# Hybrid decoder block on one core: reordered last down-projection group with interleaved stores, and a new opening around the meta tokens

## What is computed

```python
hs = concatenate([meta_tokens, x])                                   # (272, 2048)
hs = hs + 0.5 * swiglu(rmsnorm(hs, ffn1_norm), w_gate, w_up, w_down)   # d_ff 5632
hs = hs + token_mixing(rmsnorm(hs, mix_norm), w_in, ..., w_out)
hs = hs + 0.5 * swiglu(rmsnorm(hs, ffn2_norm), w_gate, w_up, w_down)
out = rmsnorm(hs, final_norm)[16:]                                   # (256, 2048)
```

## Time and profile before

| | us |
|---|---|
| median of 3 runs | 1904.35 (1903.69 to 1904.44) |
| the profiled execution | 1904.94 |
| its span, first to last event | 1902.9 |
| PE busy in it | 1878.2 |
| DVE busy | 1121.6 |
| ACT busy | 922.6 |
| POOL busy | 22.2 |
| moved by DMA | 342.21 MB |

### The profile page before, as it was taken

How to read it: one execution, slowest core, us unless ns; L and a number is a source line. 1 busy time by engine, 2 the same in 40 slices (tenths; PEclk the granted TensorE clock), 3 DMA queues, 4 the chain that set the end, 5 groups by cost and what they waited for, 6 DMA issues and landing times.

```text
span 1902.9 us, 31295 instructions
## 1 busy us (share of the span) xinstructions
PE 1878.2 (99%) x12639; PEld 1751.7 (92%) x12639; DVE 1121.6 (59%) x1212; ACT 922.6 (48%) x1176; POOL 22.2 (1%) x33
## 2 busy tenths in 40 slices
PE   8999999999999999999999999999999999999997
PEld 7999999999999999999998788888888888888886
DVE  6555555555554544468898998555566555544443
ACT  6434433443443444359888665444444444433443
POOL 4000000000000000000000000000000000000000
PEclk9999999999999999999999999999999999999999
DMA  6655555555555565555655566666656666666663
GB/s 196 189 176 176 170 173 176 172 172 175 176 171 174 177 174 172 175 175 169 186 182 168 163 191 191 193 187 188 188 176 187 188 196 189 212 187 187 189 189 121
DMA packets 283387, 342.21 MB, mean 180 GB/s; under 512 B 10656, under 2 KB 223746, under 8 KB 283169
## 3 DMA queue, kind: packets, MB, share of 16 engines
q1 hardware_dynamic: 282960, 340.83, 58.7%
q0 software_dynamic: 288, 0.19, 0.0%
q10 hardware_dynamic: 64, 0.14, 0.0%
HBM read 339.02 MB, written 2.10 MB: 179 GB/s over the span
## 4 chain that ended last, share of the span: by engine, by line
PE 96%; DVE 2%; ACT 1%; DMA 0%; issue 0%; ACTq 0%; DVEq 0%
PE ps L451 20%; PE ps L446 17%; PE ps L444 17%; PE ps L445 17%; PE ps L452 10%; PE ps L547 4%; PE ps L545 4%; PE ps L546 4%; DVE w_lo L806 1%; PE ps L404 0%; PE ps L555 0%; DMA m_tok<-in_meta_tokens 0%; DVE res L939 0%; DVE ln_sum L1003 0%; DVE res L932 0%; DVE y_f L921 0%
## 5 line engine op out<-in xcount | busy, mean ns | idle before, releaser
L806 DVE TENSOR_TENSOR w_lo<-raw,w_hi 128x1024 fp32r<-128x1024 f32 x640 | 784.4, 1227 | 660.7 <-ACT w_hi L609 658.9
L609 ACT ACTIVATE w_hi<-raw 128x1024 fp32r<-128x1024 f32 x640 | 676.5, 1059 | 862.7 <-PE ps L446 493.2
L444 PE MATMUL ps<-x_both,w_hi 128*128 128x272 f32 (+1 forms) x1920 | 555.2, 289 | 0.0
L446 PE MATMUL ps<-x_both,w_lo 128*128 128x272 f32 (+1 forms) x1920 | 554.3, 289 | 0.0
L445 PE MATMUL ps<-x_both,w_hi 128*128 128x272 f32 (+1 forms) x1920 | 551.8, 287 | 0.0
L451 PE MATMUL ps<-x_both,w_hi 128*128 128x512 f32 x1536 | 537.0, 393 | 0.5 <-DVE w_lo L806 0.5
L452 PE MATMUL ps<-x_both,w_lo 128*128 128x256 f32 x1536 | 430.9, 281 | 0.0
L445 PEld LDWEIGHTS ps<-x_both,w_hi 128*128 128x128 f32 x1920 | 362.6, 189 | 0.1
L444 PEld LDWEIGHTS ps<-x_both,w_hi 128*128 128x128 f32 x1920 | 361.9, 188 | 0.1
L446 PEld LDWEIGHTS ps<-x_both,w_lo 128*128 128x128 f32 x1920 | 361.8, 188 | 0.0
L451 PEld LDWEIGHTS ps<-x_both,w_hi 128*128 128x128 f32 x1536 | 288.3, 188 | 66.6 <-DVE w_lo L806 0.9
(11 more groups left out here) (129 smaller groups left out, 1074.2 us busy)
## 6 DMA issues: line engine op xcount, KB each, us to landing
raw<-in_ffn_w_gate SPq DMA_DIRECT2D x176, 512.0 KB, 3.7
raw<-in_ffn_w_up SPq DMA_DIRECT2D x176, 512.0 KB, 3.6
raw<-in_ffn_w_down SPq DMA_DIRECT2D x176, 512.0 KB, 3.8
raw<-in_w_in SPq DMA_DIRECT2D x80, 512.0 KB, 3.5
raw<-in_w_out SPq DMA_DIRECT2D x32, 512.0 KB, 4.7
x_tok<-in_x SPq DMA_DIRECT2D x4, 512.0 KB, 9.5
out_y<-o_tok SPq DMA_DIRECT2D x8, 256.0 KB, 3.6
gain_tok<-in_final_norm SPq DMA_DIRECT2D x1, 1024.0 KB, 4.6
```

What stands on the lines that cost most here:

```text
L444: pe.matmul(dst, w_high, act_high, start=first, stop=False)
L446: return pe.matmul(dst, w_low, act_high, start=False, stop=last)
L609: act.activation(w_hi[s][:, :], raw[s][:, :], ACT.Copy).then_inc(hi_ready, 1)
L806: dve.tensor_tensor(w_lo[s][:, :], raw[s][:, :], w_hi[s][:, :].bitcast(F32), ALU.subtract).then_inc(lo_ready, 1)
```

## The change

Two places change. At the opening the meta tokens are loaded by two DMAs at the head of SP's queue into 128 partitions (`m_rows`, chunk and token together) and turned by two transposes; x is turned two chunks at a time (`turn_pair`), four chunks before the first projection matmul and the other twelve after blocks 0, 1 and 3; block 0 is loaded and split in two halves; x's four quarters are issued before blocks 0, 2 and 4; PE runs 16 matmuls of the ones tile in three bursts (`keep_warm`); the opening group's matmuls run chunk by chunk; squares are taken of the untransposed x by ACT with an accumulator and spread on a diagonal by DVE; the parameter loads wait for x's second quarter and are turned after block 5. In the last group of `down2` the last four blocks are run for token half 0 first and then for half 1; each half has its own variance, root and scaling; half 0 is stored in two pieces of 512 KB by SP, half 1 in four of 256 KB, two by SP and two by ACT. The early Sqrt is gone. Declarations of semaphores are left out below, long removed parts too (they stand above), and indentation is reduced.

```diff
+x_sums, meta_sum = tok[:, 0:3, :].rearrange("p s h -> p h s"), tok[:, 3, 0:1]
...
-m_tok = at("m_tok", a_at + 4 * HALVES * D, [P, D])
+m_rows = at("m_rows", a_at + 4 * HALVES * D, [P, HALVES, P])
...
 out_pieces = [slice(g * BANK, (g + 1) * BANK) for g in range(G_D)]
-start_squares = [buffer[:, j, :] for buffer in (sq, t1, t2) for j in range(2)]
+wide_pieces = [slice(g * 2 * BANK, (g + 1) * 2 * BANK) for g in range(G_D // 2)]
+HALF_BLOCK = slice(0, BLOCK // 2), slice(BLOCK // 2, BLOCK)
...
+    for h in range(HALVES):
+        meta_half = meta_tokens[:, h * (D // 2):(h + 1) * (D // 2)]
+        sp.dma_start(m_rows[:, h, :],
+                     meta_half.rearrange("t (c p) -> c t p", p=P)).then_inc(meta_loaded, 16)
...
+    def load_first(src):
+        dst = raw[0][:, :].rearrange("p (c n) -> p c n", c=4)
+        for half in range(2):
+            sp.dma_start(dst[:, 2 * half:2 * half + 2, :],
+                         src[:, 2 * half:2 * half + 2, :]).then_inc(first_loaded[half], 16)
...
-                if phase == "gu1" and isinstance(g, int) and g == 0 and i < 4:
-                    load_x(i)
+                if phase == "gu1" and isinstance(g, int) and g == 0:
+                    for q in {0: (0,), 2: (1,), 4: (2, 3)}.get(i, ()):
+                        load_x(q)
                 src = rows[i % 2][i // 2, :, :, bass.ds(g * 256 + (col_a, col_b)[i % 2], 256)]
-                load(phase, g, i, src, 256)
+                if phase == "gu1" and isinstance(g, int) and g == 0 and i == 0:
+                    load_first(src)
+                else:
+                    load(phase, g, i, src, 256)
...
-    for i, cols in enumerate(out_pieces):
...
+    for i in range(2):
+        sp.wait_ge(o_scaled, 2 * i + 2)
+        sp.dma_start(out[0, 0:P, wide_pieces[i]], o_tok[:, 0, wide_pieces[i]]).then_inc(stored, 16)
+    for i in range(2):
+        sp.wait_ge(o_scaled, SET + i + 1)
+        sp.dma_start(out[0, P:2 * P, out_pieces[i]], o_tok[:, 1, out_pieces[i]]).then_inc(stored, 16)
+    sp.wait_ge(stored, 16 * 6)
 @block.gpsimd
...
+    pool.wait_ge(x_loaded[1], 16)
...
-    pool.wait_ge(sq_ready["start"], 1)
...
-    def turn_x(c, bank):
...
+    def turn_pair(q):
+        if q % 2 == 0:
+            pe.wait_ge(x_loaded[q // 2], 16)
+        if q >= 3:
+            pe.wait_ge(emptied, 2 * (q - 2))
+        for c in (2 * q, 2 * q + 1):
+            for h in range(HALVES):
+                at_col = c % 2 * SEQ + h * P
+                m = pe.transpose(ps[:, 4 + q % 3, at_col:at_col + P], x_tok[:, h, c * P:(c + 1) * P],
+                                 ident[:, :])
+        m.then_inc(x_turned, 2)
     def start_between(i):
-        if i == 1:
+        if i in (0, 1, 3):
+            for q in {0: (2, 3), 1: (4, 5), 3: (6, 7)}[i]:
+                turn_pair(q)
+        if i == 5:
             pe.wait_ge(par_loaded, 16 * (len(rows0) + 4))
-            pe.wait_ge(emptied, 5)
+            pe.wait_ge(emptied, KD)
...
-            for c in (8, 9, 10, 11):
...
+    pe.wait_ge(ones_set, 1)
+    def keep_warm(n):
+        for _ in range(n):
+            pe.matmul(ps[:, 0, 0:P], ones[:, :], ones[:, :], start=True, stop=True)
+    keep_warm(7)
...
-    pe.transpose(ps[:, 7, 0:KD], gain_rows[:, :], ident[0:KD, 0:KD]).then_inc(gain_turned, 1)
...
+    pe.transpose(ps[:, 3, 0:KD], gain_rows[:, :], ident[0:KD, 0:KD]).then_inc(gain_turned, 1)
+    pe.wait_ge(meta_loaded, 16 * HALVES)
+    for h in range(HALVES):
+        m = pe.transpose(ps[:, 7, h * P:(h + 1) * P], m_rows[:, h, :], ident[:, :])
+    m.then_inc(meta_turned, 1)
+    keep_warm(5)
+    for q in (0, 1):
+        turn_pair(q)
+    keep_warm(4)
...
     def start_group(phase, g):
-        if phase == "gu1" and isinstance(g, int) and g == 0:
-            pe.wait_ge(emptied, SET)
-        else:
+        if phase != "gu1" or not isinstance(g, int) or g > 0:
...
     def square_sums(norm, phase):
-        pe.wait_ge(sum_ready[norm], KD)
+        pe.wait_ge(sum_ready[norm], 5 if norm == "start" else KD)
...
+                if norm == "start":
+                    pe.wait_ge(par_ready, 4)
...
-                start_block(phase, g, i)
-                for j in range(2):
-                    for c in range(4):
+                opening = norm == "start" and first_group
+                if opening and i == 0:
+                    pe.wait_ge(first_lo, 1)
+                else:
+                    start_block(phase, g, i)
+                for j, c in ([(j, c) for c in range(4) for j in range(2)] if opening
+                             else [(j, c) for j in range(2) for c in range(4)]):
...
+                        if opening and i == 0 and c == 2 and j == 0:
+                            start_block(phase, g, i)
...
         pe.wait_ge(emptied, banks_before("gu2", G_FF - 1) if g < G_D // 2 else banks_before("down2", 0))
-        for i in range(N_DOWN):
...
+        def half_block(i, h):
+                s = slot("down2", g, i)
...
-                if g == G_D - 1 and i == N_DOWN - 1 and h == 0:
-                    m.then_inc(tile_done, 1)
+                return m
+        split = N_DOWN - RING if g == G_D - 1 else N_DOWN
+        for i in range(split):
+            start_block("down2", g, i)
+            if g == 0:
+                pe.wait_ge(alo_ready["gu2"], i + 1)
+            for h in range(HALVES):
+                m = half_block(i, h)
...
+        if split < N_DOWN:
+            for h in range(HALVES):
+                for i in range(split, N_DOWN):
+                    if h == 0:
+                        start_block("down2", g, i)
+                    m = half_block(i, h)
+                m.then_inc(tile_done, 1)
    ...
-    act.dma_start(m_tok[0:META, :], meta_tokens).then_inc(x_loaded[4], 16)
...
-        act.wait_ge(raw_loaded[s], 16 * turn(phase, g, i) + 16)
+        act.wait_ge(raw_loaded[s], 16 * turn(phase, g, i) + (16 if s else 0))
...
-        act.wait_ge(emptied, t + 1 if norm == "start" else banks_before(norm, 0) + t + 1)
+        act.wait_ge(emptied, 2 * (t // 2) + 2 if norm == "start" else banks_before(norm, 0) + t + 1)
...
+    def square_x(h, half):
+        act.wait_ge(x_loaded[2 * half + 1], 16)
+        act.activation(t12[:, :, :].rearrange("p a t -> p (a t)")[:, 0:D // 2],
+                       x_tok[:, h, half * (D // 2):(half + 1) * (D // 2)], ACT.Square,
+                       accum_out=x_sums[:, h, half:half + 1]).then_inc(x_squared, 1)
     act.wait_ge(gain_turned, 1)
-    act.activation(gain1[:, :], ps[:, 7, 0:KD], ACT.Copy).then_inc(gain_ready, 1)
+    act.activation(gain1[:, :], ps[:, 3, 0:KD], ACT.Copy).then_inc(gain_ready, 1)
     act.wait_ge(gain_ready, 1)
-    for q in range(4):
+    act.wait_ge(first_loaded[0], 16)
+    act.activation(w_hi[0][:, HALF_BLOCK[0]], raw[0][:, HALF_BLOCK[0]], ACT.Copy).then_inc(first_hi, 1)
+    act.wait_ge(meta_ready, 1)
+    for t in (0, 1):
+        operand("gu1", "start", t)
+    act.wait_ge(first_loaded[1], 16)
+    act.activation(w_hi[0][:, HALF_BLOCK[1]], raw[0][:, HALF_BLOCK[1]], ACT.Copy).then_inc(hi_ready, 1)
+    for t in (2, 3):
+        operand("gu1", "start", t)
+    high("gu1", 0, 1)
+    for q in range(1, 4):
...
-        high("gu1", 0, 2 * q + 1)
...
+        if q == 3:
+            high("gu1", 0, 7)
         if q == 1:
-            act.wait_ge(par_turned, 4)
...
+            act.wait_ge(meta_loaded, 16 * HALVES)
+            act.activation(t12[:, 0, 0:HALVES * P], m_rows[:, :, :].rearrange("p h n -> p (h n)"),
+                           ACT.Square, accum_out=meta_sum).then_inc(x_squared, 1)
+            act.wait_ge(x_squared, 1)
+            square_x(0, 0)
+        if q == 2:
+            act.wait_ge(x_squared, 2)
+            square_x(1, 0)
+        if q == 3:
+            for h in range(HALVES):
+                act.wait_ge(x_squared, 3 + h)
+                square_x(h, 1)
+        else:
+            high("gu1", 0, 2 * q + 1)
+    act.wait_ge(par_turned, 4)
+    for s in range(4):
+        act.activation(par[:, s, 0:n_rows[s]], ps[:, 4, s * P:s * P + n_rows[s]],
+                       ACT.Copy).then_inc(par_ready, 1)
...
-    act.activation(step[:, 1, 0:1], step[:, 0, 0:1], ACT.Sqrt)
...
+    for h in range(HALVES):
+        act.wait_ge(tile_done, h + 1)
+        token_squares(G_D - 1, h)
+        act.wait_ge(last_var, h + 1)
+        act.activation(tok[:, 1, h:h + 1], tok[:, 0, h:h + 1], ACT.Sqrt).then_inc(last_sd, 1)
+    act.wait_ge(last_newton[1], 4)
+    act.wait_ge(tok_read, HALVES * G_D)
+    for cols in out_pieces[2:]:
+        act.activation(o_tok[:, 1, cols], o_tok[:, 1, cols], ACT.Copy,
+                       scale=tok[:, 3, 1:2]).then_inc(o_scaled_s, 1)
+    for i, cols in enumerate(out_pieces[2:]):
+        act.wait_ge(o_scaled_s, i + 1)
+        act.dma_start(out[0, P:2 * P, cols], o_tok[:, 1, cols]).then_inc(stored, 16)
 @block.vector
...
-    for q in range(4):
...
+    def copy_pair(q):
+        dve.wait_ge(x_turned, 2 * q + 2)
+        dve.tensor_copy(res[:, 2 * q:2 * q + 2, META:T],
```

(98 more changed lines are left out.)

63 lines of the change are left out of this document (2 added, 61 removed).

## The result

| | before | after |
|---|---|---|
| median, us | 1904.11 (4 runs, 1903.69 to 1904.44) | 1892.79 (4 runs, 1892.61 to 1893.15) |
| the profiled execution | 1904.94 | 1892.61 |
| its span | 1902.9 | 1890.8 |
| PE's last matmul done | 1891.6 | 1883.0 |
| from there to the end | 11.3 | 7.8 |

The ratio is 0.9941 (95% interval 0.9924 to 0.9958): 11.3 us faster, where 9.3 were forecast. The last two rows are of the profiled executions. In a second series of five runs the changed kernel had a median of 1893.82 beside 1904.32, 10.5 us faster.

The account below looks back on a forecast made before the run. PE was taken to bound the middle, leaving only start and end: opening 4.5 + 1.3 - 0.2 = 5.6 us plus end 3.7 makes 9.3, so 1904.35 - 9.3 = 1895.1 us; range 1893.5 to 1898.3.

Parts of the forecast that it names:

- x's first quarter, 7.07: Opening: x's first quarter, issued at 1.77 us and landing 5.3 later, starts the transposes at 7.07 instead of 8.12.
- The rival of a late x at 8.4: Opening: meta loads on half the DMA engines delay x's first quarter to 8.4 us, giving 1896.4 us; chance 13%.
- Meta tokens, 4.7, and 4.6 at the earliest: Opening: second half of the meta tokens, loaded first on SP's queue, lands at 4.7 us, at the earliest 4.6.
- First matmul, 10.4: Opening: first projection matmul at 10.4 us, X + 3.35, instead of 14.89; gain 4.5 us.
- Clock, 1.3: Opening: bursts of ones-matmuls raise the clock early, so 13 matmuls take 0.126 instead of 0.227 us; gain 1.3 us.
- high from about 5 on: Opening: PE runs real matmuls from 1.0 to 4.1 us and again from about 5, the clock staying high from then.
- comparison with 3 us of real matmuls: Opening: the first burst lasts as long as the 3 us of real matmuls after which the clock rose before.
- gaps of 2 to 3 us against the 4 us of the earlier trace: Opening: remaining PE gaps of 2 to 3 us are shorter than the 4 us before the clock fell at the end.
- Transposes, a cost of 0.2: Opening: 24 x transposes in the stream at 0.185 us make 4.4 us against 4.2 before; cost 0.2 us.
- The end, 3.7: After PE's last matmul: 7.0 to 8.3 us instead of 11.3; gain 3.7 us, bounds 3.0 and 4.3.
- the landmarks T - 1.5, T - 0.7, T + 2.7: End, T being the last matmul's end: half 0's two wide stores at T - 1.5 and T - 0.7, half 1's first at T + 2.7.
- Squares, parameters, loads, block supply: nothing: Opening and last group: sums ready at about 34.6 us, wanted at 36.1; parameters there by 24, wanted at about 33; no stalls.

Follow-up runs that it names:

- the repeat: The changed kernel run and profiled once more without an edit, on the same chip as the last three variants: 1893.82 us, ratio 0.9945.

## Why the prediction was wrong

**The bottom of it stood.** What bounds, and where, was read rightly: the chain is PE from the first matmul to T, and both ends moved by the mechanisms named. One term of the opening was mis-sized, and the range had no room for it. Point by point:

- *x's first quarter, 7.07.* Measured 6.97 and, in the repeat, 7.19. Two small errors met: the two meta issues take 0.78 and 0.61 us and not 0.5 each, so x is issued at 2.26, and lands 4.7 to 5.1 later and not 5.3; that they nearly cancel is luck. The rival of a late x at 8.4 did not come.
- *Meta tokens, 4.7, and 4.6 at the earliest.* That bound was wrong: in the run without bursts PE waited for them and ran their first transpose at 4.09. Nothing hung on it, since with the bursts PE came to them at 4.5 to 4.6.
- *First matmul, 10.4.* 10.19, in the repeat 10.40. Its steps (copies of 0.65 to 0.7, 0.60 for half of w_lo, 0.42 for x_lo) were right.
- *Clock, 1.3.* Right in size. The step "high from about 5 on" held in the first trace, but only just: in five of the eight traces the rise came at 5.9 to 6.7 us, and the run with the first burst alone shows that the comparison with 3 us of real matmuls was not enough to bank on. The other comparison, gaps of 2 to 3 us against the 4 us of the earlier trace rows, was no margin either. In the changed kernel's first trace T is 1883.0, and the windows behind it give (columns as in the earlier trace rows):

```profile
1879.00:1886.00 7.00, 4.01 (x18) 3.00 (x16) 4.77 (x19) 2.35 (x7) 0.00 (x0) 0.94 0.37 150
1886.00:1888.00 2.00, 0.00 (x0) 0.00 (x0) 0.22 (x1) 0.67 (x2) 0.00 (x0) 0.50 0.67 250
```

  A mean of 0.94 over 7 us puts the fall to 0.50 at about 1885.1, 2.1 us after PE's last matmul; in the run without bursts it came 5.2 us after it. That the clock stayed up through the opening's gaps in all eight traces is therefore an outcome with some luck in it, not something the rows had secured. Without any burst the loss is 2.1 us.
- *Transposes, a cost of 0.2.* **This is the step that failed.** I took 0.37 / 2 = 0.185 us for an x transpose at the high clock from a stretch in which a 16-row transpose stood between each two chunks, and carried it over into a stretch without them. Without them an x transpose takes 0.109 us: each group of eight takes 0.87 us, 2.6 in all instead of the 4.4 forecast, against 4.2 before: a gain of 1.6, an error of 1.8 us. The run with the 16-row transposes put back brings the 0.37 back, and the run with them grouped puts 0.25 us on each change to 16 rows and back. So 0.076 of the forecast's 0.185 us a transpose belonged to the neighbours.
- *The end, 3.7.* 3.5; the landmarks T - 1.5, T - 0.7, T + 2.7 came out at T - 1.4, T - 0.7, T + 2.8.
- *Squares, parameters, loads, block supply: nothing.* So it was. DVE had the sums formed by about 32.3 (34.6 in the forecast), PE asked at 34.69; PE's parameter transposes followed block 5 without a wait.
- *Range.* Its lower end was made of x's landing and of the end, the two terms that turned out right, and had no bound below for the price of the transposes, though nothing excluded a gain there. 9.3 + 1.8 gives 11.1 us, or 1893.25 us, still outside, and the two series measured 11.3 and 10.5. The pace of out_cf, 0.9 us from one execution to the next in the same code, wasn't in it at all; with it alone the range would have reached down to 1892.6. The 2.0 us outside the span, taken as unchanged, became 1.8.

## What to carry to other kernels

A duration read from a mixed stretch is a duration of the mixture: ask what stands between the instructions before using it for a stretch from which the neighbours are gone. Issue a small load that starts the work ahead of the large ones, in as few issues as it can be made; on another queue, behind them, it landed when they did. To overlap the end of a kernel, split the last group early enough for the first half's whole chain, in-order engines and table loads too, to be over before the second half asks for them. Two blocks were too few here and four were enough; more were not tried.

## What the runs showed of the hardware

- Among fp32 transposes at the high clock, going from 128-row ones to a 16-row one and back costs about 0.25 us; the 16-row transpose itself costs 0.06, a 128-row one 0.109.
- 128 KB issued on ACT's queue just behind 512 KB of x on SP's landed 6.9 us after their issue (one load, 16 partitions); in two loads of 64 KB on 128 partitions they were complete 9.0 us after the first issue and 7.8 after the second. At the head of SP's queue the same bytes were there within 3.3 us of the first issue (PE, waiting for them, ran at 4.09 in the run without bursts).
- One burst of seven fp32 matmuls, 3.4 us long, was followed by transposes at the low level 2.7 us later and real matmuls at the low level 6.6 us later; with bursts of 7, 5 and 4, and gaps of up to 1.2 us between them and x's transposes, x's transposes and the real matmuls ran at the high level in each of the eight traces in which the bursts stood where the change puts them. The rise came anywhere from 4.3 to 6.7 us after the start. At the end of the kernel the fall came 2.1 us after the last matmul in one trace and 5.2 in another.
- The second half of the same 256 pairs of 512- and 256-column matmuls ran at either of two paces, 0.353 and 0.346 us a pair, that differ from one execution to the next.
- The table load for the square root took 1.28 us, and the square root ran 0.02 us behind it.
